# Router logits from stationary router weights in four column quarters, and the first token gather taken straight from the slot table

## The reference

```python
x = layer_norm(ALPHA * x + mix, ln1_g[l], ln1_b[l])            # x1, 1024 x 1024
aff = jax.nn.sigmoid(jnp.dot(xt, router_w))                     # logits: 1024 x 16
sel_score = aff + router_bias                                   # best group of 4, then the top 2 experts in it
...
h = silu(einsum('cd,edf->cef', xc, w_gate)) * einsum('cd,edf->cef', xc, w_up)
h = h * gc[:, :, None]                                          # gate of each token and expert
return einsum('cef,efd->cd', h, w_down)
```

## Time and profile before

| | us |
|---|---|
| median of 3 runs (lowest, highest) | 1038.42 (1037.26, 1040.1) |
| the profiled execution, its own time | 1040.04 |
| its span, first to last instruction | 1038.3 |
| PE busy | 930.5 |
| DVE busy | 686.0 |
| ACT busy | 558.8 |
| POOL busy | 365.1 |

### The profile page before, as it was taken

The page is one execution under the profiler, slowest core; times in us unless marked ns, Lnnn a source line. Parts: engine busy times, 40 slices in busy tenths (PEclk is TensorE's granted clock), DMA queues, the critical chain, the costliest instruction groups (busy, mean ns, idle before and its releaser), DMA issues.

```text
span 1038.3 us, 15787 instructions
## 1 busy us (share of the span) xinstructions
PE 930.5 (90%) x4784; PEld 734.6 (71%) x4785; DVE 686.0 (66%) x998; ACT 558.8 (54%) x794; POOL 365.1 (35%) x231
## 2 busy tenths in 40 slices
PE   7999999999888899999927999999999999999820
PEld 5877888643565568888926888888888888888720
DVE  4339888897999754646575757888888834314326
ACT  3356576786685665601222647777777734324323
POOL 0000089999999970000001112222323311111116
PEclk8999999999899898999957999999999999999965
DMA  8450111000000100525545679999999897433164
GB/s 227 119 148 21 41 42 62 1 1 0 1 2 1 42 1 21 182 92 222 198 178 205 243 236 334 390 404 383 405 383 405 315 357 232 133 65 97 40 174 190
DMA packets 60972, 171.14 MB, mean 165 GB/s; under 512 B 17120, under 2 KB 31456, under 8 KB 48608
## 3 DMA queue, kind: packets, MB, share of 16 engines
q1 hardware_dynamic: 53584, 143.85, 37.4%
q0 software_dynamic: 7056, 25.69, 10.3%
q10 hardware_dynamic: 288, 1.05, 0.3%
HBM read 141.73 MB, written 26.21 MB: 162 GB/s over the span
## 4 chain that ended last, share of the span: by engine, by line
PE 70%; DVE 12%; DMA 9%; ACT 4%; issue 3%; ACTq 0%; DVEq 0%; POOLq 0%; POOL 0%; SPq 0%
PE ps L449 17%; PE ps L451 16%; PE ps L450 16%; DMA raw<-in_w_gate 8%; PE ps L701 4%; PE ps L747 3%; PE ps L780 3%; DVE wlo L1635 2%; PE ps L767 2%; PE ps L833 2%; PE ps L888 1%; ACT whi L1160 1%; DVE bias L1305 1%; DVE probs L1432 1%; DVE sm L1485 1%
## 5 line engine op out<-in xcount | busy, mean ns | idle before, releaser
L1635 DVE TENSOR_TENSOR wlo<-raw,whi 128x2048 fp32r<-128x2048 f32 x96 | 216.1, 2288 | 50.5 <-ACT whi L1160 50.4
L1160 ACT CAST whi<-raw 128x2048 fp32r<-128x2048 f32 x96 | 179.9, 1912 | 44.4 <-DMA raw<-in_w_gate 17.5
L449 PE MATMUL ps<-whi,xgT_hi 128*128 128x512 f32 x384 | 153.2, 399 | 6.7 <-DVE xgT_lo L1645 6.4
L451 PE MATMUL ps<-whi,xgT_lo 128*128 128x512 f32 x384 | 150.8, 393 | 0.0
L450 PE MATMUL ps<-wlo,xgT_hi 128*128 128x512 f32 x384 | 150.7, 392 | 0.0
L1731 POOL TENSOR_SCALAR tapped<-hpad,par 128x1024 f32<-128x1024 f32 x30 | 92.0, 3067 | 2.9
L449 PE MATMUL ps<-xT_hi,w_hi 128*128 128x512 f32 (+1 forms) x224 | 87.8, 392 | 4.8 <-DVE w_lo L1249 3.1
L449 PEld LDWEIGHTS ps<-whi,xgT_hi 128*128 128x128 f32 x384 | 73.0, 190 | 22.8 <-issue 5.3
L450 PE MATMUL ps<-xT_lo,w_hi 128*128 128x512 f32 (+1 forms) x224 | 86.9, 388 | 0.0
L451 PE MATMUL ps<-xT_hi,w_lo 128*128 128x512 f32 (+1 forms) x224 | 86.8, 387 | 0.0
L1796 POOL COPY idx_now<-slot_token 128x1 int32 (+1 forms) x24 | 8.9, 370 | 220.4 <-PE ps L888 220.4
(11 more groups left out here) (286 smaller groups left out, 1854.8 us busy)
## 6 DMA issues: line engine op xcount, KB each, us to landing
raw<-in_w_gate SPq DMA_DIRECT2D x32, 1024.0 KB, 10.7
raw<-in_w_up SPq DMA_DIRECT2D x32, 1024.0 KB, 11.9
raw<-in_w_down SPq DMA_DIRECT2D x32, 1024.0 KB, 10.1
w_raw<-in_w_in SPq DMA_DIRECT2D x14, 512.0 KB, 4.0
x_tok<-in_x SPq DMA_DIRECT2D x8, 512.0 KB, 7.9
wo_raw<-in_w_o SPq DMA_DIRECT2D x16, 256.0 KB, 2.9
x_res<-in_x SPq DMA_DIRECT2D x16, 256.0 KB, 3.4
x_d<-xa SPq DMA_DIRECT2D x4, 512.0 KB, 6.0
```

Source lines behind the costliest of these rows:

```text
L449: pe.matmul(out, l_hi, r_hi, start=start, stop=False)
L451: return pe.matmul(out, l_lo, r_hi, start=False, stop=stop)
L1160: act.copy(whi[:, n, :], raw[:, n, :]).then_inc(gu_hi if n < 4 else dn_hi, 1)
L1635: dve.tensor_tensor(wlo[:, n, :], raw[:, n, :], f32(whi[:, n, :]), ALU.subtract).then_inc(gu_lo if n < 4 else dn_lo, 1)
```

## The change

1. `rw_wide` is a copy of the router weights with each 128x16 piece padded to 128x32, and `fold` is a 128x16 sum of four shifted identities. POOL makes both after its convolution work, behind the waits `searched` and `route_in`, and signals `router_set`, for which PE now waits ahead of the second half of `W_o`.
2. `logits(t)` makes `rw_wide[:, k]` stationary (32 columns) and moves 128 tokens of `x1T`. Piece k goes to partitions 32g to 32g+31 of bank 2, g = k mod 4, so two pieces are summed in each quarter. ACT copies the 128x128 partial sums to `parts` (`parts_copy`), and `logits_sum(t)` is one matmul with `parts` stationary and `fold` moving, which adds the quarters and gives tokens on the partitions in bank 3.
3. In the loop the transposes now lag one tile behind `W_o` (before: two), the logits two (three), the sums three. ACT's copies lag accordingly.
4. POOL no longer copies the index for the first gather; the DMA reads column 0 of `slot_token`.
5. PE transposes the first gathered tile ahead of the gate table's matmuls, and DVE takes the tile's low part right after `split([0])`, then the gate table, then `split([1, 2, 3])`.

```diff
             def logits(t):
                 pe.wait_ge(x1T_set, 2 * t + 2)
+                if t:
+                    pe.wait_ge(part_set, t)
                 for k in range(KT):
-                    last = pe.matmul(ps[:, 2, t * 16:(t + 1) * 16], x1T[k // 4][:, k % 4, t * P:(t + 1) * P], rw[:, k, :],
-                                     start=k == 0, stop=k == KT - 1)
-                last.then_inc(lg_mm, 1)
+                    g = k % 4
+                    last = pe.matmul(ps[32 * g:32 * g + 32, 2, 0:P], rw_wide[:, k, :], x1T[k // 4][:, k % 4, t * P:(t + 1) * P],
+                                     start=k < 4, stop=k >= 4)
+                last.then_inc(part_mm, 1)
+            def logits_sum(t):
+                pe.wait_ge(part_set, t + 1)
+                pe.matmul(ps[:, 3, t * 16:(t + 1) * 16], parts[t % 2][:], fold[:], start=True, stop=True).then_inc(lg_mm, 1)
...
-            pe.wait_ge(route_in, 32)
+            pe.wait_ge(router_set, 1)
...
                 last.then_inc(wo_mm, 1)
+                if t >= 1:
+                    x1_transposes(t - 1)
                 if t >= 2:
-                    x1_transposes(t - 2)
+                    logits(t - 2)
                 if t >= 3:
-                    logits(t - 3)
-            for t in range(NT - 2, NT):
-                x1_transposes(t)
-                logits(t - 1)
+                    logits_sum(t - 3)
+            logits(NT - 2)
+            for t in range(NT - 3, NT - 1):
+                logits_sum(t)
+            x1_transposes(NT - 1)
             logits(NT - 1)
+            logits_sum(NT - 1)
...
+            def parts_copy(t):
+                act.wait_ge(part_mm, t + 1)
+                if t >= 2:
+                    act.wait_ge(lg_mm, t - 1)
+                act.copy(parts[t % 2][:], ps[:, 2, 0:P]).then_inc(part_set, 1)
             for t in range(NT):
+                if t >= 1:
+                    x1T_copy(t - 1)
                 if t >= 2:
-                    x1T_copy(t - 2)
+                    parts_copy(t - 2)
                 act.wait_ge(stat1, 3 * t + 3)
...
-            for t in range(NT - 2, NT):
-                x1T_copy(t)
+            parts_copy(NT - 2)
+            x1T_copy(NT - 1)
+            parts_copy(NT - 1)
...
             split([0], 0)
+            x_lo_part(0)
             gate_table()
-            split([1], 0)
-            x_lo_part(0)
-            split([2, 3], 0)
+            split([1, 2, 3], 0)
...
+            pool.wait_ge(searched, 1)
+            pool.wait_ge(route_in, 32)
+            pool.tensor_tensor(fold[:], ident[:, 0:EXPERTS], ident[:, 32:32 + EXPERTS], ALU.add)
+            link(pool.memset(rw_wide[:], 0.0))
+            for g in range(2, 4):
+                link(pool.tensor_tensor(fold[:], fold[:], ident[:, 32 * g:32 * g + EXPERTS], ALU.add))
+            pool.tensor_copy(rw_wide[:, :, 0:EXPERTS], rw).then_inc(router_set, 1)
...
-            pool.wait_ge(table_set, 1)
-            pool.tensor_copy(idx_now[:], slot_token[:, 0:1]).then_inc(idx0_set, 1)
             pool.wait_ge(x1_out, 16 * NT)
             pool.wait_ge(spare_rows, 32)
-            pool.wait_ge(idx0_set, 1)
-            pool.indirect_dma_start(xg[:], None, x1_d, bass.IndirectOffsetOnAxis(ap=idx_now[:], axis=0)
+            pool.wait_ge(table_set, 1)
+            pool.indirect_dma_start(xg[:], None, x1_d, bass.IndirectOffsetOnAxis(ap=slot_token[:, 0:1], axis=0)
```

More of the change, by code:

```diff
@@ L307, in program @@
         sm = at("sm", [P, 432], F32, END + 2)
+        fold = at("fold", [P, EXPERTS], F32, END + 0.4375)
+        rw_wide = at("rw_wide", [P, KT, 32], F32, END + 0.5)
+        parts = [at(f"parts{i}", [P, P], F32, CST + 11 + 0.5 * i) for i in range(2)]
         iw = sm[:, 0:64].rearrange("p (t h) -> p t h", t=NT)
@@ L426, in program @@
         route_in, lg_mm, aff_set = sem("route_in"), sem("lg_mm"), sem("aff_set")
+        router_set, part_mm, part_set = sem("router_set"), sem("part_mm"), sem("part_set")
         oh_set, count_mm, rank_mm = (sem(n) for n in ("oh_set", "count_mm", "rank_mm"))
@@ L877, in _ @@
             last.then_inc(table_mm, 1)
-            pe.wait_ge(gate_hot, 1)
-            for n in range(2 * NT):
-                last = pe.matmul(ps[:, 7, 0:3 * (TILES + 1)], slot_row[:, n, :],
-                                 gate_col[:, n].rearrange("p c t -> p (c t)"), start=n == 0, stop=n == 2 * NT - 1)
-            last.then_inc(gate_mm, 1)
             def xgT(t):
@@ L929, in _ @@
             xgT(0)
+            pe.wait_ge(gate_hot, 1)
+            for n in range(2 * NT):
+                last = pe.matmul(ps[:, 7, 0:3 * (TILES + 1)], slot_row[:, n, :],
+                                 gate_col[:, n].rearrange("p c t -> p (c t)"), start=n == 0, stop=n == 2 * NT - 1)
+            last.then_inc(gate_mm, 1)
             gate_up(0, 0)
@@ L1137, in norm @@
                 act.activation(x, x, ACT.Identity, bias=shift, scale=rstd).then_inc(ln_unit, 1)
+            def parts_copy(t):
[3 more added lines that the diff above has]
+                act.copy(parts[t % 2][:], ps[:, 2, 0:P]).then_inc(part_set, 1)
             for t in range(NT):
+                if t >= 1:
+                    x1T_copy(t - 1)
                 if t >= 2:
-                    x1T_copy(t - 2)
+                    parts_copy(t - 2)
                 act.wait_ge(stat1, 3 * t + 3)
                 act.activation(sd1[:, t:t + 1], mv1[:, t, 1:2], ACT.Sqrt, bias=eps).then_inc(ln1_sd, 1)
-            for t in range(NT - 2, NT):
-                x1T_copy(t)
+            parts_copy(NT - 2)
+            x1T_copy(NT - 1)
+            parts_copy(NT - 1)
             act.wait_ge(lg_mm, NT)
             act.wait_ge(wo_mm, 2 * NT)
-            act.activation(aff, ps[:, 2, 0:128], ACT.Sigmoid).then_inc(aff_set, 1)
+            act.activation(aff, ps[:, 3, 0:128], ACT.Sigmoid).then_inc(aff_set, 1)
             def split(t, pieces, loaded):
```

## The result

The changed kernel takes **1026.29 us**, the median of 9 runs (1023.3 to 1032.28); the kernel before took 1038.42 on the same chip (9 runs, 1034.08 to 1040.77). The ratio is 0.9894, with a 95% interval of 0.9869 to 0.9918: 11 us less, 8.5 to 13.6 (it is the ratio of the means; the medians lie 12.1 apart). The profiled execution has a span of 1024.2 us against 1038.3, 14.1 less.

A forecast was written before the change was run, and what follows sets the result against it. PE was taken to bound the kernel, directly or held up by chains of other engines. Gains of 0.28 + 0.15 + 2.39 + 0.74 + 0.37 = 3.93 us from the 1038.42 median gave 1034.5 us; own range 1033.5 to 1036.5, overall 1030.3 to 1037.5.

The forecast's parts named there:

- What a logits record costs: PE's router logits: a record on four quarters costs 0.055 us, between bounds of 0.109 (no overlap) and 0.027.
- The term of the tile: PE's logits of one tile, without the sum: 16 records at 0.055 plus 0.09 for entering column mode, 0.97 us.
- In the loop: Second W_o half, PE work ahead of its last matmul: 6.84 us becomes 6.56, gain 0.3 (bounds -4.0 to +2.5).
- Ahead of tile 7's transposes: Behind the last W_o matmul: PE's remaining work fits into DVE's 5.2 us; transposes start 0.15 us earlier (0 to 0.3).
- From M to the sigmoid: M is the start of tile 7's transposes; the sigmoid comes at M + 6.23 instead of M + 8.62, gain 2.4 us.
- all of this part is at the lower clock level: From the last W_o matmul to the sigmoid, PE was taken to run at 1.2 GHz (granted 0.50).
- The table load on the path: ACT_TABLE_LOAD, 1.28 us, stands behind the last parts_copy, no longer hidden by the logits, and eats 0.6 us of gain.
- The gather's start: Without POOL's copy the first gather's DMA starts 0.83 us behind slot_token: gain 0.74 us (0 to 1.5).
- DVE's order: Ahead of gate_up(0): DVE's low part no longer waits for split([1]), which comes later: gain 0.37 us.
- from there on the expert loop shifts as a whole: From gate_up(0) on, the expert loop was only to start earlier, with no gain of its own.
- The third rival: The clock: PE holds 2.4 GHz until the sigmoid, giving 1032.8 us, or rises sooner in gate_up(0), unpriced; chance 0.15.
- four quarters at a time: First rival, on the logits: all four quarters overlap, 2.2 us more in the loop, 0.8 in the tail: 1031.5; chance 0.20.

The follow-up runs named there:

- the run with pairs: Changed kernel with two neighbouring pieces in a row on each quarter instead of g = k mod 4: 1025.87 us, ratio 0.9885.
- the one profile with both waits filled: Changed kernel, sigmoid table loaded before the last x1T copy, unread matmuls filling PE's waits around tile 7's transposes and before gate_up(0): 1027.42 us, ratio 0.9896.
- the run with the early table: Changed kernel plus a one-column sigmoid on ACT that loads the activation table ahead of the last x1T copy: 1029.86 us, ratio 0.9913.

## Why the prediction was wrong

The mechanism was right, the size was not: every stretch in the forecast's sum moved the way that it said, and 5.9 us more were gained there than it had. By its steps:

- **What a logits record costs: the step that failed first.** I had the bounds right (0.109 and 0.027) and chose 0.055 by a reason about the order of the passes that nothing in the trace bore. The record costs 0.027, and the run with pairs shows that the order doesn't matter. The term of the tile, 0.97, measured 0.66: entering at 0.09 was right, and the records with the exit were 0.57 and not 0.88. Of this 0.57 the exit, which I had at nothing by a misreading of the earlier trace rows, is 0.09. The sum's two records took 477.77 - 477.53 = 0.24 for my 0.21.
- **In the loop**, forecast 0.28: with these terms it is 6.84 - (5 x 0.66 + 4 x 0.24 + 0.87) = 1.71, and 1.65 was measured. The new waits and POOL's operations cost nothing, as said: PE has no gap there.
- **Ahead of tile 7's transposes**, forecast 0.15: 0.27, and PE waited there for DVE for 1.72 us.
- **From M to the sigmoid**, forecast M + 6.23: M + 4.54. The 1.69 us have two causes. The step "all of this part is at the lower clock level" failed: the transposes ran at 2.4 GHz, and ACT's copy of `x1T` ended at 511.19 + 1.07, M + 1.76, not M + 2.57, which is 0.81. And from that copy to the start of the table load I had 6.21 - 1.28 - 2.57 = 2.36, and it was 513.75 - 512.26 = 1.49, which is 0.87: the record's price again (16 took 1.08 and not 2.00). The table load on the path, at 0.6 us, was right.
- **The way of the gather** took 4.47 us for 4.68, of which I had nothing; in the kernels with the new order it took 4.40 to 5.04, and I can't say what the 0.21 are.
- **The gather's start**, forecast 0.74 by a gap of 0.83: the gap was 534.17 - 533.24 = 0.93, the same as behind the copy, and 0.64 was gained. DVE's order gave 0.33 for 0.37.
- **`gate_up(0)`** had no term: 2.62 us. The sum said "from there on the expert loop shifts as a whole". The third rival named the sooner rise of the clock, but priced only the tail. I had the granted clock of 0.50 over 553 to 559 before me, and the change moves 1.5 us of PE work into the idle right ahead of it. The price of a rise at the start stands in the same row: 6 us of PE at half the clock are 3 us of work at the full one.

Of the rivals, four quarters at a time was the right one, at 0.20, and the clock, at 0.15, the other, though not as priced: of its 1.7 us in the tail 0.8 came, since the logits still ran at 1.2 GHz, and the sooner rise in `gate_up(0)`, which it named without a price, brought 2.6. That this profile had all 2.6 was in part luck: four of the eight with this order and the same idle time had half of it or less. The quarters and the clock came together, and their sum, which the text named as 1029.8 and then cut off as a corner, still lacked `gate_up(0)`. Put into my sum, the measured stretches give 1040.04 - 9.8 = 1030.2 for the profiled execution, and 1028.6 by the median shown. The 1026.29 of the runs lies 2.3 us below that, which is inside the interval of the ratio, and which no stretch of the change explains.

## What to carry to other kernels

Where a matmul's stationary operand has few columns, spread the matmuls over all column quarters: the cost of a record is that of the full width divided by the quarters in use, in both orders tried, plus 0.09 us to enter and 0.09 to leave. Count what folds the quarters together as well, here a copy on ACT and 0.24 us of PE a tile. Where nothing in a trace shows a price, a reason for a value between the bounds is no measurement; keep the bound's chance as high as the reason is untested. Look for stretches at the lower clock on the path, and cost what an edit does to PE's idle time ahead of them, not only to the work in them: here 3.4 of 9.8 us were clock (0.8 in the tail, 2.6 in `gate_up(0)`).

## What the runs showed of the hardware

- A float32 record of 128 moving columns costs 0.027, 0.055 and 0.109 us with four, two and one column quarters, by their starts. Records for a free quarter start ahead of earlier ones in program order (inferred from the run in pairs). At 1.2 GHz the 16 on four quarters took 1.08 us, as long as 16 on two at 2.4.
- From a record at full width to one on a column quarter or half, and back, PE takes 0.09 us more from start to start than between two at full width, with one, two or four quarters in use.
- The clock fell in the kernel before while PE was busy without a gap: from 510.73 to 515.35 its rows are records of 16 moving columns, but for one tile's transposes, and the fall came at 514.72. In the changed kernel PE waited 1.72 us ahead of M, and the level fell 1.1 us behind M; with this wait and the next filled it held to M + 4.7. So a full row of busy tenths didn't keep the level, and in the one profile with both waits filled it stayed longer.
- The same rows on PE were followed by a rise 3.7 us behind the start of tile 0's transposes in the changed kernel (542.3) and 7.6 us behind it in the run with the early table (547.4): 11.19 and 12.53 us for the same 48 matmuls.
- The first indirect DMA started 0.93 us behind the end of what it waited for, whether POOL itself had written the indices (before) or DVE (after).
